# Turning the last hidden tile of a feed-forward block: its second token block on VectorE instead of TensorE

## What is computed

```python
def _swiglu(h, w_gate_up, w_down):                  # block 0
    g, u = jnp.split(h @ w_gate_up, 2, axis=-1)
    return (jax.nn.silu(g) * u) @ w_down

def swiglu(x, w1, w3, w2):                          # blocks 1 to 4
    return (jax.nn.silu(x @ w1) * (x @ w3)) @ w2
def post_norm(x, sub, g, b):
    return layer_norm(DN_ALPHA * x + sub, g, b)
# used as  h = post_norm(h, 0.5 * swiglu(h, w1, w3, w2), g, b)
```

## Time and profile before

| | |
|---|---|
| median of 3 runs | 1464.09 (1463.18 to 1464.46) |
| the profiled execution, its own time | 1463.24 |
| its span | 1461.5 |
| TensorE busy | 1442.2, 99% of the span |
| VectorE busy | 1088.2, 74% |
| ScalarE busy | 688.1, 47% |
| GpSimd busy | 206.9, 14% |
| granted TensorE clock | 0.999 |
| matmuls of line 1070 | 20, 271 ns each, 3.8 busy |
| 32x128 turns of line 2399 | 800, 303 ns each, 242.2 busy |

### The profile page before, as it was taken

How to read it: one execution, slowest core, us unless ns; L and a number is a source line. 1 busy time by engine, 2 the same in 40 slices (tenths; PEclk the granted TensorE clock), 3 DMA queues, 4 the chain that set the end, 5 groups by cost and what they waited for, 6 DMA issues and landing times.

```text
span 1461.5 us, 20857 instructions
## 1 busy us (share of the span) xinstructions
PE 1442.2 (99%) x7488; PEld 1219.0 (83%) x7488; DVE 1088.2 (74%) x1825; ACT 688.1 (47%) x854; POOL 206.9 (14%) x189
## 2 busy tenths in 40 slices
PE   9999999999999999999999999999999999999997
PEld 8988897888888888889988888898888897788886
DVE  5765757888778877757758877777887777688876
ACT  5346556444444444454435443465444377444442
POOL 1073011200001000300032000301000335510001
PEclk9999999999999999999999999999999999999999
DMA  8754553855656556565567556576556450465561
GB/s 279 240 173 144 197 175 124 295 189 183 213 185 210 172 189 212 173 207 197 172 203 238 172 197 206 172 246 212 175 185 214 146 180 30 134 238 175 182 214 64
DMA packets 198876, 274.48 MB, mean 188 GB/s; under 512 B 9632, under 2 KB 158240, under 8 KB 198560
## 3 DMA queue, kind: packets, MB, share of 16 engines
q1 hardware_dynamic: 194304, 256.62, 53.3%
q0 software_dynamic: 4368, 16.78, 3.2%
q10 hardware_dynamic: 144, 0.26, 0.0%
HBM read 272.32 MB, written 1.31 MB: 187 GB/s over the span
## 4 chain that ended last, share of the span: by engine, by line
PE 89%; DVE 4%; POOL 3%; ACT 3%; issue 1%; DMA 0%; DVEq 0%; SPq 0%; ACTq 0%; POOLq 0%
PE ps L646 25%; PE ps L648 25%; PE ps L647 25%; PE ps L758 3%; PE ps L752 3%; PE ps L741 3%; PE ps L687 1%; ACT whi L1415 1%; POOL wlo L2763 1%; DVE wlo L1986 1%; PE ps L805 1%; PE ps L1126 0%; PE ps L1254 0%; DVE big L2587 0%; POOL big L2808 0%
## 5 line engine op out<-in xcount | busy, mean ns | idle before, releaser
L1986 DVE TENSOR_TENSOR wlo<-raw,whi 128x2048 fp32r<-128x2048 f32 (+1 forms) x224 | 509.4, 2291 | 167.7 <-ACT whi L1415 165.7
L1415 ACT CAST whi<-raw 128x2048 fp32r<-128x2048 f32 (+1 forms) x239 | 452.8, 1894 | 372.5 <-PE ps L648 327.5
L646 PE MATMUL ps<-whi,st_hi 128*128 128x512 f32 (+1 forms) x1064 | 414.7, 390 | 0.0
L648 PE MATMUL ps<-whi,st_lo 128*128 128x512 f32 (+1 forms) x1064 | 412.5, 388 | 0.0
L647 PE MATMUL ps<-wlo,st_hi 128*128 128x512 f32 (+1 forms) x1064 | 412.4, 388 | 0.0
L2399 DVE STREAM_TRANSPOSE hidT<-hidden 32x128 f32<-32x128 f32 x800 | 242.2, 303 | 12.3
L648 PEld LDWEIGHTS ps<-whi,st_lo 128*128 128x128 f32 (+1 forms) x1064 | 198.9, 187 | 41.2
L646 PEld LDWEIGHTS ps<-whi,st_hi 128*128 128x128 f32 (+1 forms) x1064 | 198.9, 187 | 40.6 <-issue 0.3
L647 PEld LDWEIGHTS ps<-wlo,st_hi 128*128 128x128 f32 (+1 forms) x1064 | 199.0, 187 | 40.1
L646 PE MATMUL ps<-whi,hid_hi 128*128 128x512 f32 x400 | 156.2, 390 | 0.0
L648 PE MATMUL ps<-whi,hid_lo 128*128 128x512 f32 x400 | 155.7, 389 | 0.0
(11 more groups left out here) (261 smaller groups left out, 1429.0 us busy)
## 6 DMA issues: line engine op xcount, KB each, us to landing
raw<-in_ffn_w SPq DMA_DIRECT2D x264, 512.0 KB, 4.8
raw<-in_w_gate_up SPq DMA_DIRECT2D x44, 512.0 KB, 4.7
raw<-in_w_in SPq DMA_DIRECT2D x32, 512.0 KB, 5.1
raw<-in_sgu_w_in SPq DMA_DIRECT2D x32, 512.0 KB, 4.6
raw<-in_w_down SPq DMA_DIRECT2D x22, 512.0 KB, 5.1
raw<-in_sgu_w_out SPq DMA_DIRECT2D x16, 512.0 KB, 4.7
raw<-in_kv_w SPq DMA_DIRECT2D x12, 512.0 KB, 4.6
raw<-in_w_proj_attn SPq DMA_DIRECT2D x8, 512.0 KB, 4.6
```

The source lines that it names most:

```text
L646: pe.matmul(o, a[0], b[0], start=start, stop=False)
L648: return pe.matmul(o, a[1], b[0], start=False, stop=stop)
L1415: act.copy(whi[:, s, 0:n], raw[:, s, 0:n]).then_inc(whi_ready, 1)
L1986: dve.tensor_tensor(wlo[:, s, 0:n], raw[:, s, 0:n], whi[:, s, 0:n].bitcast(F32), ALU.subtract).then_inc(wlo_ready, 1)
```

## The change

The turn of token block 1 in the last step is taken from TensorE. VectorE does it with 16 instructions of 32x64 from `hidden` into the second half of `hidT`. ScalarE rounds from `hidT` in place of PSUM, VectorE subtracts from `hidT` and raises `hid_ready`, for which TensorE now waits before the last 12 matmuls. On VectorE the turn and `hidden_last(1)` stand ahead of the subtraction of the next unit. Token block 0 is as it was. The counts of `hid_count` rise by one for each block.

```diff
             plan_split(("hid", n), FSTEPS - 1)
-            for tb in range(2):
-                plan(("hid_last", n, tb), 6 + tb, split=True)
+            plan(("hid_last", n, 0), 6, split=True)
+            plan_split(("hid_last", n, 1))
...
-            return (FSTEPS - 1) * n + i + 1
+            return FSTEPS * n + i + 1
...
                 gate_up(i, u0 + 2, i - 1)
-                turn_last(0)
+                turn_last()
                 pe.wait_ge(hid_ready, hid_count(n, i - 1))
                 w_before = down_weights(u0 + 4, i - 1)
                 down_block(w_before, hid_hi, hid_lo, 0)
-                turn_last(1)
                 w_last = down_weights(u0 + 3 * FSTEPS - 1, 0)
                 last = [x[:, 8:10, :] for x in (st_hi, st_lo)]
                 pe.wait_ge(*read(("hid_last", n, 0)))
                 down_block(w_last, *last, 0, end=True)
                 down_block(w_before, hid_hi, hid_lo, 1).then_inc(w_used, 1)
-                pe.wait_ge(*read(("hid_last", n, 1)))
+                pe.wait_ge(hid_ready, hid_count(n, i))
                 down_block(w_last, *last, 1, end=True, ahead=ahead).then_inc(w_used, 1)
...
                 def hidden_last(tb):
                     key = ("hid_last", n, tb)
-                    act.wait_ge(*full(key))
-                    act.copy(st_hi[:, 8:10, tb * P:tb * P + P],
-                             bank(key)[:, 0:2 * P].rearrange("p (f t) -> p f t", f=2)).then_inc(hi_rounded, 1)
+                    if tb:
+                        act.wait_ge(hid_turned, hid_count(n, FSTEPS - 1))
+                        src = hidT[:, :, P:2 * P]
+                    else:
+                        act.wait_ge(*full(key))
+                        src = bank(key)[:, 0:2 * P].rearrange("p (f t) -> p f t", f=2)
+                    act.copy(st_hi[:, 8:10, tb * P:tb * P + P], src).then_inc(hi_rounded, 1)
...
+                def turn_last():
+
+                    dve.wait_ge(*read(("up", n, 1), FSTEPS - 1))
+                    for a in range(4):
+                        for b in range(4):
+                            src = view(hidden[32 * a:32 * a + 32, 1, 32 * b:32 * b + 1], (P, 2), (1, 32))
+                            dst = view(hidT[32 * b:32 * b + 32, 0, P + 32 * a:P + 32 * a + 1], (S, 2), (1, 32))
+                            mm = dve.transpose(dst, src)
+                    mm.then_inc(hid_turned, 1)
...
                 hidden_in(FSTEPS - 1)
                 hidden_last(0)
+                turn_last()
+                hidden_last(1)
                 upto(last + 1)
-                hidden_last(1)
```

More of the change, by code:

```diff
@@ L1063, in down @@
                     down_block(w, hid_hi, hid_lo, 1, start).then_inc(w_used, 1)
-                def turn_last(tb):
-                    key = ("hid_last", n, tb)
-                    pe.wait_ge(*read(up[tb], FSTEPS - 1))
+                def turn_last():
+                    key = ("hid_last", n, 0)
+                    pe.wait_ge(*read(up[0], FSTEPS - 1))
                     room(key)
                     for f in range(2):
-                        mm = pe.transpose(bank(key)[:, f * P:f * P + P], hidden[:, tb, f * P:f * P + P], ident)
+                        mm = pe.transpose(bank(key)[:, f * P:f * P + P], hidden[:, 0, f * P:f * P + P], ident)
                     mm.then_inc(*is_full(key))
@@ L2405, in hidden_last @@
                     hi, lo = (x[:, 8:10, tb * P:tb * P + P] for x in (st_hi, st_lo))
-                    dve.tensor_tensor(lo, bank(key)[:, 0:2 * P].rearrange("p (f t) -> p f t", f=2), hi.bitcast(F32),
-                                      ALU.subtract).then_inc(*is_read(key))
+                    if tb:
+                        dve.tensor_tensor(lo, hidT[:, :, P:2 * P], hi.bitcast(F32), ALU.subtract).then_inc(hid_ready, 1)
+                    else:
+                        dve.tensor_tensor(lo, bank(key)[:, 0:2 * P].rearrange("p (f t) -> p f t", f=2), hi.bitcast(F32),
+                                          ALU.subtract).then_inc(*is_read(key))
                 def hidden_out(i):
```

## The result

| | before | changed |
|---|---|---|
| median of 4 runs | 1463.99 (1463.18 to 1464.46) | 1484.69 (1483.89 to 1485.97) |
| ratio, 95% interval | | 1.0143 (1.0132 to 1.0155) |
| profiled execution, its own time | 1463.24 | 1483.89 |
| its span | 1461.5 | 1482.2 |
| mean granted TensorE clock | 0.999 | 0.991 |

The forecast was 1466.0, the range ended at 1469.2. The change costs 20.7 us, eleven times the sum of the prediction.

A forecast was written before the change was run, and what follows sets the result against it. TensorE, busy 99% of the span, was taken to bound the kernel, with VectorE making its next input at block ends. Blocks 2, 1, 4, 0, 3 gave 1.05 + 0.71 + 0.54 - 0.22 - 0.22 = +1.9 on 1464.09: 1466.0 us, range 1463.0 to 1469.2.

The forecast's parts named there:

- the forecast fit: End of block 0: `res` ready at 429.75, just before TensorE would turn it at 429.77, keeping TensorE's 0.22 us gain.
- d = 1.41: Block ends, VectorE: the norm starts at T + 6.21 instead of T + 4.80, a delay of 1.41 us.
- T: The start of TensorE's first turn in a block, from which times at that block's end are counted; 929.41 in block 2.
- VectorE subtracts from T + 5.86 for 0.41: Block ends: VectorE's subtraction of the turned tile, after turn and rounding, starts at T + 5.86 and takes 0.41 us.
- d - 0.36: End of block 2: the norm's delay less 0.36 us of idle time before `st_lo`, a cost of 1.05 us.
- d - 0.70: End of block 1: the norm's delay less 0.70 us hidden by GpSimd's late root, a cost of 0.71 us.
- Block 3's slack of 3.3 us: End of block 3: `res` is done 3.3 us before TensorE turns it, so the block gains 0.22 us.
- The second wait in block 1: GpSimd makes token block 1's root only after its weight unit, from 616.77; variance ready at 616.07, hiding 0.70 us of delay.
- `hid_ready` with its slack: TensorE's new wait before its last 12 matmuls in a block has 2.1 us of slack and costs nothing.
- 1475 or more, `hid_ready` late: Rival: turns end 2.1 us later than thought, at a step of 0.39, and all five blocks pay; chance 0.03.
- The next (1470.2): Rival: VectorE's turns cost their full width, a step of 0.316 and d = 2.47, +6.1 us in all; chance 0.17.
- the hidden case: Rival: VectorE's delay is hidden and only TensorE's gain remains, -1.1 us, 1463.0; needs d under 0.1; chance 0.10.

The follow-up runs named there:

- Experiments 2 and 3: Kernel before the change, TensorE still turning both token blocks, with 14 and 16 unused turns added on VectorE: 1464.55 us (ratio 1.0002) and 1477.13 us (1.0086).
- experiment 7: Changed kernel, with VectorE's turns written to PSUM and read there, and GpSimd's second weight unit waiting for `res` of token block 0: 1468.75 us, ratio 1.0032.

## Why the prediction was wrong, step by step

- **Removed, 0.22 us for each block: right.** Block 0 ends 0.25 us earlier, and there the forecast fit held: TensorE turned `res` at 429.74 (before at 429.99), with no idle time before it.
- **16 turns at 236 ns, 3.99 us: right** (236 and 3.98). Half the width saved the 67 ns worked out from two widths of another operation.
- **The rounding of 0.39: right** (0.407).
- **d = 1.41: close where nothing was held.** In block 4 the norm started 6.08 us after T, 1.28 late; the first turn followed the subtraction before it without the tenth of a microsecond that I had put between. The cost there was 0.26 where 0.54 was forecast.
- **"VectorE subtracts from T + 5.86 for 0.41": this step failed.** The prediction took its duration from rows of `st_lo<-ps,st_hi`, an instruction with one input in PSUM. The changed one reads two from SBUF while GpSimd does the same, and took 1.91 in the blocks 1, 2 and 3 (0.42 in 0 and 4). This is what I did not cost at all: the change moved an operand from PSUM to SBUF.
- **"What is queued behind on VectorE does cost", with the sums d - 0.36 and d - 0.70: this failed by far more.** They let the chain behind move by d with each duration kept. But the two writes of `res` had stood just ahead of GpSimd's second unit, the second of them with some 0.65 us to spare. Experiments 2 and 3 bracket that: 14 unused turns cost 0.5 us, 16 cost 13.0. Any d over that margin turned 1.42 us into over 5.5. Block 3's slack of 3.3 us went the same way: TensorE waited 3.19 us there. With both holds taken away (experiment 7) the loss was 4.5, not 1.9, so the sum itself was not confirmed to the microsecond; that kernel differs also in its turns into PSUM and its later weight unit.
- **The second wait in block 1 (GpSimd's root behind its unit)** never came to bear. GpSimd made the root of token block 0 later, went on to its unit at once, and had been done for 5 us when the variance of token block 1 came.
- **`hid_ready` with its slack: right.** TensorE did not wait before its last 12 matmuls, though the hold left some 0.8 us of the 2.1 in block 1 (the tile was ready at T + 7.65).
- **The rivals** did not hold the cause. The one that names such a time (1475 or more, `hid_ready` late) needed turns 0.39 apart and a wait before the last 12 matmuls; neither came, so that its time was met says nothing for it. The next (1470.2) rested on the price of the turn. Against the hidden case the prediction said that no instruction of VectorE falls much under 150 ns; the kernel before has some of 80 ns (reading an accumulator), so that argument was wrong, though the measured 236 ns rules the case out. The full-width price at d = 2.47 would in truth have been over the margin as well, like the forecast itself.

The bound from the rows was no bound: it enclosed the price of the new instruction, but not what others would cost beside it.

## What to carry to other kernels

When VectorE's work moves in time, or an operand moves from PSUM to SBUF, lay GpSimd's instructions beside it: here VectorE's instructions with two SBUF inputs, and a float32 copy and a `tensor_scalar` too, stood still until GpSimd's 4.6 us instruction ended. A chain with slack against the engine that it feeds can have far less against such a neighbour; count the distance to GpSimd's next start before moving anything by more than that. An instruction whose duration differs from that of its twins with the same shape is the trace's sign of it, and is to be explained before the forecast.

## What the runs showed of the hardware that I had not expected

- The hold goes both ways and follows the start: with 14 unused turns GpSimd's unit took 4.89 us in place of 4.63 when it started 0.4 us before a two-input instruction of VectorE ended; in the changed kernel nearly the same overlap cost 0.10.
- A float32 copy and a `tensor_scalar` of 128x256 with one SBUF tensor were held for 4.21 us. 32x64 turns and statistics (`BATCH_NORM_STATS2`) beside the same unit took their usual time.
- A 32x64 turn takes 236 ns into SBUF and 256 ns into PSUM.
- In block 1 of the changed kernel a stall of 6.7 us left TensorE at the lower clock for 6 us of full work behind it, in block 2 a stall of the same length for 3.4 us (955.14 to 958.50, granted clock 0.50). After the 1.49 us stall of experiment 7 the mean clock of the whole execution was 0.998.
